# Two layer changes: three quarters of the layer norm's scaling on GpSimd, and other orders on ScalarE and VectorE

## The reference

```
def _layernorm(x, w, b):
    xf = x.astype(jnp.float32)
    mu = jnp.mean(xf, axis=-1, keepdims=True)
    var = jnp.mean(jnp.square(xf - mu), axis=-1, keepdims=True)
    return ((xf - mu) * lax.rsqrt(var + EPS)).astype(x.dtype) * w + b

for layer in range(DEPTH):
    y = _mla_mixer(x, ...) if layer % N_MIXERS == 0 else _mlstm_mixer(x, ...)
    x = _layernorm(ALPHA * x + y, ln_w[layer], ln_b[layer])
```

## Time and profile before

| What | us |
|---|---|
| median of 3 runs (1819.11 to 1819.42) | 1819.4 |
| the profiled execution's own time | 1819.39 |
| its span, first to last instruction | 1817.7 |
| TensorE busy in the span | 1803.0 |
| VectorE busy | 1270.0 |
| ScalarE busy | 942.8 |
| GpSimd busy | 37.8 |

### The profile page before, as it was taken

The page is one execution under the profiler, slowest core; times in us unless marked ns, Lnnn a source line. Parts: engine busy times, 40 slices in busy tenths (PEclk is TensorE's granted clock), DMA queues, the critical chain, the costliest instruction groups (busy, mean ns, idle before and its releaser), DMA issues.

```text
span 1817.7 us, 24358 instructions
## 1 busy us (share of the span) xinstructions
PE 1803.0 (99%) x8863; PEld 1518.4 (84%) x8863; DVE 1270.0 (70%) x1720; ACT 942.8 (52%) x1310; POOL 37.8 (2%) x116
## 2 busy tenths in 40 slices
PE   8999999999999999999999999999999999999999
PEld 7899998878888888887888888888878888888887
DVE  6766766588556755767887878787786556577764
ACT  4555554455465555636655545554454444565542
POOL 2000000000000004000000000000000000000000
PEclk9999999999999999999999999999999999999999
DMA  8554454668889887575555564544776776555453
GB/s 295 172 176 149 136 176 155 204 179 188 182 151 211 176 179 175 192 238 161 171 177 151 164 183 150 175 152 159 235 208 209 214 218 207 160 164 161 162 165 114
DMA packets 175067, 326.72 MB, mean 180 GB/s; under 512 B 16824, under 2 KB 24912, under 8 KB 174208
## 3 DMA queue, kind: packets, MB, share of 16 engines
q1 hardware_dynamic: 173840, 321.04, 61.6%
q10 hardware_dynamic: 576, 4.19, 0.6%
q0 software_dynamic: 560, 0.26, 0.1%
HBM read 319.68 MB, written 5.77 MB: 179 GB/s over the span
## 4 chain that ended last, share of the span: by engine, by line
PE 98%; DVE 1%; ACT 1%; issue 0%; DMA 0%; DVEq 0%
PE acc L388 28%; PE acc L390 28%; PE acc L389 28%; PE ps L650 2%; PE ps L2921 2%; PE ps L498 1%; PE acc L354 1%; PE acc L355 1%; PE acc L353 1%; PE ps L683 1%; PE acc L341 0%; PE acc L371 0%; PE acc L372 0%; PE acc L375 0%; PE acc L377 0%; PE acc L370 0%
## 5 line engine op out<-in xcount | busy, mean ns | idle before, releaser
L324 DVE TENSOR_TENSOR wsp<-wraw,wsp 128x1024 fp32r<-128x1024 f32 x576 | 696.6, 1224 | 334.1 <-ACT wsp L304 331.3
L304 ACT ACTIVATE wsp<-wraw 128x1024 fp32r<-128x1024 f32 x576 | 597.6, 1053 | 369.7 <-PE acc L390 337.4
L388 PE MATMUL acc<-wsp,ta 128*128 128x512 f32 x1664 | 659.3, 396 | 4.5 <-DVE wsp L324 2.4
L390 PE MATMUL acc<-wsp,ta 128*128 128x512 f32 x1664 | 649.2, 390 | 0.0
L389 PE MATMUL acc<-wsp,ta 128*128 128x512 f32 x1664 | 647.7, 389 | 0.0
L388 PEld LDWEIGHTS acc<-wsp,ta 128*128 128x128 f32 x1664 | 312.6, 188 | 69.8 <-issue 4.3
L390 PEld LDWEIGHTS acc<-wsp,ta 128*128 128x128 f32 x1664 | 312.3, 188 | 66.8
L389 PEld LDWEIGHTS acc<-wsp,ta 128*128 128x128 f32 x1664 | 312.8, 188 | 62.4
L388 PE MATMUL acc<-wsp,tb_hi 128*128 128x512 f32 x576 | 228.2, 396 | 0.0
L390 PE MATMUL acc<-wsp,tb_lo 128*128 128x512 f32 x576 | 224.8, 390 | 0.0
L389 PE MATMUL acc<-wsp,tb_hi 128*128 128x512 f32 x576 | 224.4, 390 | 0.0
(11 more groups left out here) (334 smaller groups left out, 1585.2 us busy)
## 6 DMA issues: line engine op xcount, KB each, us to landing
wraw<-in_ml_w_in SPq DMA_DIRECT2D x129, 512.0 KB, 5.7
wraw<-in_a_w_in SPq DMA_DIRECT2D x128, 512.0 KB, 3.8
wraw<-in_kv_w SPq DMA_DIRECT2D x64, 512.0 KB, 4.4
wraw<-in_b_w_in SPq DMA_DIRECT2D x64, 512.0 KB, 4.3
wraw<-in_mla_w_in SPq DMA_DIRECT2D x49, 512.0 KB, 4.6
wraw<-in_mla_w_out SPq DMA_DIRECT2D x32, 512.0 KB, 4.1
wraw<-in_ml_w_out SPq DMA_DIRECT2D x32, 512.0 KB, 4.6
wraw<-in_a_w_out SPq DMA_DIRECT2D x32, 512.0 KB, 4.0
```

The costliest lines, as they stand in the source:

```text
L304: nc.scalar.activation(unit_of(whi, n, SPLIT, w), unit_of(wraw, n, RAW, w), ACT.Copy).then_inc(w_high, 1)
L324: nc.vector.tensor_tensor(unit_of(wlo, n, SPLIT, w), unit_of(wraw, n, RAW, w), unit_of(whi, n, SPLIT, w).bitcast(F32), ALU.subtract).then_ ...
L388: nc.tensor.matmul(o, xh, wh, start=first, stop=False)
L390: m = nc.tensor.matmul(o, xl, wh, start=False, stop=end)
```

## The change

Both layer changes are edited alike; the arithmetic is the same.

- `ln_scale` on VectorE now does quarter 0 only. A new `ln_scale` on GpSimd does quarters 1 to 3 as three instructions of 128x512, each raising the new semaphore `xn_rest`; it waits for `nrm_a`. GpSimd does (0, 0) and (0, 1) ahead of its pads and mask, and (1, 0) and (1, 1) behind the masks of the third layer.
- TensorE's `ln_turn` waits for `xn_ok` for quarter 0 and for `xn_rest` for quarters 1 to 3. `ln_stream` waits for both.
- ScalarE makes the high half of unit 2 behind hi(0, 0) instead of ahead of affine(0, 0).
- VectorE does `ln_stats` of block 1 behind the low half of unit 2, directly ahead of `ln_scale(n, 1)`, instead of between unit 1 and lo(0, 1); the scale of quarters 1 to 3 of block 1, which stood behind unit 3, is gone from its queue.
- In `head_norm` of the last layer two semaphores become one; ScalarE's wait has the same meaning.

```diff
--- before.py
+++ after.py
@@ -163,6 +163,7 @@
         lnp_in = sem("lnp_in")
 
         nrm_a, nrm_v, xn_ok = sem("nrm_a"), sem("nrm_v"), sem("xn_ok")
+        xn_rest = sem("xn_rest")
         st_out = sem("st_out")
 
 
@@ -969,7 +970,7 @@
 
 
 
-        l3 = sems(3, "r_dg r_row f_row f_e f_ok sq_out x_sq x_out x_in x_tmp x_hi x_lo kss qss oss ksq kv_ krs kn kt kT qsq qv qrs qn qt qT sc msk mx ex pt ptc pv o "
+        l3 = sems(3, "r_dg r_row f_row f_e f_ok sq_out x_sq x_out x_in x_tmp x_hi x_lo ksq kv_ krs kn kt kT qsq qv qrs qn qt qT sc msk mx ex pt ptc pv o "
                      "ge gs sq v rs on og ogp tmp hi lo")
 
         def dst_l3(name, k, b, it):
@@ -1189,6 +1190,17 @@
                 pool.dma_start(gbias[:, 1:2], a["kv_f_bias_2"].rearrange("(n o) -> n o", o=1)).then_inc(bias_in, 16)
             pool.dma_start(posi, a["positions"][0:1, :].to_broadcast([P, T])).then_inc(bias_in, 16)
 
+            def ln_scale(n, b):
+
+
+                pool.wait_ge(nrm_a, 2 * n + b + 1)
+                for q in range(1, 4):
+                    x = x_res[:, b, q * COLS:(q + 1) * COLS]
+                    nc.gpsimd.tensor_scalar(x, x, mv[:, b, 0:1], nrm[:, b, 2:3], ALU.subtract,
+                                            ALU.mult).then_inc(xn_rest, 1)
+
+            ln_scale(0, 0)
+            ln_scale(0, 1)
             pool.wait_ge(xn_ok, 1)
             own.mark(nc.gpsimd.memset(cin[:, :, 0:PAD], 0.0))
             own.mark(nc.gpsimd.memset(mask[:], 0.0))
@@ -1223,6 +1235,9 @@
                 nc.gpsimd.tensor_copy(lvl[:, i, :].rearrange("p (m t) -> p m t", t=P),
                                       lvf.unsqueeze(1).to_broadcast([P, 4, P])).then_inc(l2["masks"], 1)
                 pool.wait_ge(l2["masks"], i + 2)
+
+            ln_scale(1, 0)
+            ln_scale(1, 1)
 
 
         @block.scalar
@@ -1358,10 +1373,11 @@
                 hi = lambda b, q: ln_hi(act, own, turn, b, q)
                 split = lambda p: step(act, high, evac, name, p)
                 ln_rstd(n, 0)
-                for p in range(3):
+                for p in range(2):
                     split(p)
                 affine(0, 0)
                 hi(0, 0)
+                split(2)
                 hi(0, 1)
                 affine(0, 2)
                 split(3)
@@ -1627,7 +1643,7 @@
                 nc.scalar.activation(ps2(2), src.rearrange("p b n -> p (b n)"), ACT.Square).then_inc(done, 1)
 
             def inverse_root(v, rs, g):
-                act.wait_ge(v, g + 1)
+                act.wait_ge(v, 2 * g + 2)
                 nc.scalar.activation(sm[:, 40:48], sm[:, 32:40], ACT.Ln).then_inc(rs, 1)
                 act.wait_ge(rs, 2 * g + 1)
                 nc.scalar.activation(sm[:, 48:56], sm[:, 40:48], ACT.Exp, scale=-0.5).then_inc(rs, 1)
@@ -1883,9 +1899,9 @@
 
             quarter = lambda q0, q1: slice(q0 * COLS, q1 * COLS)
 
-            def ln_scale(n, b, q0, q1):
-
-                c = quarter(q0, q1)
+            def ln_scale(n, b):
+
+                c = quarter(0, 1)
                 dve.wait_ge(nrm_a, 2 * n + b + 1)
                 nc.vector.tensor_scalar(x_res[:, b, c], x_res[:, b, c], mv[:, b, 0:1], nrm[:, b, 2:3],
                                         ALU.subtract, ALU.mult).then_inc(xn_ok, 1)
@@ -1896,7 +1912,8 @@
                 half = len(pieces) // 2
                 if i == 0:
                     dve.wait_ge(lnp_in, 32 * (n + 1))
-                    dve.wait_ge(xn_ok, 4 * n + 4)
+                    dve.wait_ge(xn_ok, 2 * n + 2)
+                    dve.wait_ge(xn_rest, 6 * n + 6)
                 piece = lambda j: (pieces[j][0], quarter(pieces[j][1], pieces[j][1] + 1))
                 if i > 0:
                     own.sync()
@@ -2031,20 +2048,18 @@
                 split = lambda p: step(dve, low, evac, name, p)
                 last_residual(done, 0)
                 ln_stats(n, done, 0)
-                ln_scale(n, 0, 0, 1)
-                ln_scale(n, 0, 1, 4)
+                ln_scale(n, 0)
                 split(0)
                 affine(0, 1)
                 last_residual(done, 1)
                 lo(0, 0)
                 split(1)
-                ln_stats(n, done, 1)
                 lo(0, 1)
                 split(2)
-                ln_scale(n, 1, 0, 1)
+                ln_stats(n, done, 1)
+                ln_scale(n, 1)
                 lo(0, 2)
                 split(3)
-                ln_scale(n, 1, 1, 4)
                 lo(0, 3)
                 lo(1, 0)
                 affine(1, 1)
@@ -2494,12 +2509,12 @@
                                                       ALU.add))
                 nc.vector.tensor_copy(negF, frow[:, 3, :]).then_inc(l3["f_ok"], 1)
 
-            def head_norm(dst, src, sq, ss, vs, rs, on, g):
+            def head_norm(dst, src, sq, vs, rs, on, g):
 
                 dve.wait_ge(sq, g + 1)
                 nc.vector.tensor_reduce(sm[:, 32:40], ps2(2).rearrange("p (n d) -> p n d", d=HD), AX,
-                                        ALU.add).then_inc(ss, 1)
-                dve.wait_ge(ss, g + 1)
+                                        ALU.add).then_inc(vs, 1)
+                dve.wait_ge(vs, 2 * g + 1)
                 nc.vector.tensor_scalar(sm[:, 32:40], sm[:, 32:40], 1.0 / HD, EPS, ALU.mult, ALU.add).then_inc(vs, 1)
                 dve.wait_ge(rs, 2 * g + 2)
                 for b in range(TB):
@@ -2548,7 +2563,7 @@
 
             def kv_side(g, p):
                 if p == late("l3_kv", 0):
-                    head_norm(qw3, qw3, l3["ksq"], l3["kss"], l3["kv_"], l3["krs"], l3["kn"], g)
+                    head_norm(qw3, qw3, l3["ksq"], l3["kv_"], l3["krs"], l3["kn"], g)
                     if not first(g):
                         dve.wait_ge(l3["kT"], 64 * g)
                     blocks = square_blocks(o3.rearrange("p b n -> p (b n)"))
@@ -2579,7 +2594,7 @@
             def q_side(g, u):
 
                 def norm():
-                    head_norm(qw3, qw3, l3["qsq"], l3["qss"], l3["qv"], l3["qrs"], l3["qn"], g)
+                    head_norm(qw3, qw3, l3["qsq"], l3["qv"], l3["qrs"], l3["qn"], g)
 
                 def out_(hh):
                     r = fox.inverse(dve, own, g, hh)
@@ -2593,7 +2608,7 @@
                     nc.vector.tensor_tensor(gw3[:, b, :], gw3[:, b, :], tmpT[:, 0, :], ALU.mult).then_inc(l3["gs"], 1)
 
                 def post():
-                    head_norm(o3, o3, l3["sq"], l3["oss"], l3["v"], l3["rs"], l3["on"], g)
+                    head_norm(o3, o3, l3["sq"], l3["v"], l3["rs"], l3["on"], g)
                     dve.wait_ge(l3["on"], 2 * g + 2)
                     dve.wait_ge(l3["gs"], 2 * g + 2)
                     flat = lambda v: v.rearrange("p b n -> p (b n)")
@@ -2755,7 +2770,10 @@
                 l0_side(3, p, l0_at("l0_out"))
             def ln_turn(n, b, q):
 
-                pe.wait_ge(xn_ok, 4 * n + 2 * b + (1 if q == 0 else 2))
+                if q == 0:
+                    pe.wait_ge(xn_ok, 2 * n + b + 1)
+                else:
+                    pe.wait_ge(xn_rest, 6 * n + 3 * b + q)
                 turn_block(x_res, b, q, n == 1 and b == 1)
 
             def ln_change(n, done, src, name):
```

## The result

The changed kernel takes **1825.69 us** (median of 7, 1825.53 to 1827.23) against 1819.42: ratio 1.0037, 95% interval 1.0027 to 1.0046. That is 6.3 us slower, above the predicted range of 1817.3 to 1823.2, and on the side of the slower rival. In the changed kernel's code all lines lie a little further down: 498 is 499, 324 is 325, 555 is 556, 583 is 584, VectorE's scale 1890 is 1906, and GpSimd's scale is 1199.

What follows compares the result with a forecast made beforehand. TensorE was taken as the bound, busy 1803.0 of 1817.7 us, with 3.54 us of pauses to win; losses of 2 x (0.19 + 0.90) = +2.2 us on 1819.4 gave 1821.6 us, range 1817.3 to 1823.2.

Steps and rivals of the forecast that it cites:

- slower rival: Block 1 ahead of unit 3: GpSimd's quarter is long, 1.16 us and fully blocked, +5.0 us, 1824.4; chance 0.14.
- ScalarE's order and VectorE until unit 2: First layer change: affine(0, 0) at 357.15, TensorE resumes at 360.40 instead of 360.94, unit 2 1.39 us earlier.
- The 0.19 stays: Unit 3 in block 1: TensorE follows at 367.03 against 366.84, so 0.19 us is lost per change, 0.38 in both.
- After this point TensorE has no wait: After unit 3 in either change: no TensorE wait today and nothing else late, so the 0.19 us loss remains.
- I take 0.61, the same shape on the same engine: GpSimd's 128x512 scale, without a trace row: assumed 0.61 us, as GpSimd's cast of 128x512.
- my upper bound of 1.16: GpSimd's 128x512 scale: at most 1.16 us, from four selects of 128x128 at 0.29 each.
- signs of being wrong: Layer changes: unit 3 no later and TensorE's idle falling, or quarters above 0.9 us and transposes waiting for GpSimd.
- Hidden, also at 0.9 us each: Block 0: GpSimd's quarters end near 356.1, 357.9 and 358.5, before TensorE wants them at about 357.0, 358.9 and 359.4.
- The collisions: Block 1, before lo(0, 2) and unit 3: GpSimd holds VectorE up twice at 0.45 us, 0.90 per change.
- the sum of 1821.6: Whole kernel: 2 x (0.19 + 0.90) = +2.2 us on 1819.4 us.
- the select's cost per element: GpSimd's select of 128x128 at 0.29 us, the evidence for a 1.16 us quarter and a kernel time of 1824.4.
- the prediction's own case: Both layer changes: GpSimd quarters of 0.61 us, two collisions of 0.45 per change, +2.2 us; chance 0.50.

Runs made afterwards that it cites:

- experiment 3: Kernel before in its own ScalarE and VectorE orders, with the scale of quarters 1 to 3 moved to GpSimd: 1825.68 us, ratio 1.0034.
- the copies: Changed kernel with GpSimd's scale of quarters 1 to 3 replaced by a copy of each quarter onto itself: 1824.49 us, ratio 1.0027.

## Why the prediction was wrong, point by point

- **ScalarE's order and VectorE until unit 2: right.** With the orders alone, 360.40 for TensorE's return and 367.05 for new(0, 3) were as worked out.
- **"The 0.19 stays": wrong, small.** The orders alone cost nothing. "After this point TensorE has no wait" overlooked that new(1, 0) hung on lo(1, 0) already, which ended at 369.7; 0.19 of slack was there. What the prediction left out is that the later root also delays GpSimd: with the three long quarters behind it, the new orders cost 1.5 us (experiment 3).
- **"I take 0.61, the same shape on the same engine": the step that failed.** Same shape, another operation. The quarter is 2.06 us, and my upper bound of 1.16 was itself built from other operations (selects). The quarters above 0.9 us and the transposes waiting for GpSimd are what the prediction had named as signs of being wrong. With 2.06, block 0's last quarter comes 6.5 us after the root where it is wanted after 4.4, and "Hidden, also at 0.9 us each" falls.
- **The collisions: right as a mechanism, mis-sized both ways.** With short instructions they cost 1.2 us per change (0.90 forecast): three collisions instead of two, since VectorE's scale was held up as well, of 0.37 to 0.40 each instead of 0.45. The cast's own row had VectorE pay 0.31 of 0.45, which makes 0.42 of a whole one. So that the estimate of 1821.3 without the clock comes so near the sum of 1821.6 is in part luck: the third collision stands in for the 0.19 that wasn't there. With the long instructions only 0.41 was lost; presumably GpSimd reached just one border between VectorE's instructions before unit 3, which no run tests. The Trainium skill (SBUF — State Buffer, Who interferes with whom) has the second instruction fully blocked. For the copies the rows go that way, with 0.37 to 0.40 of the 0.61. Beside the 2.06 us scale they don't: lo(0, 0) and unit 1 kept 0.68 and 1.22. Beside the scale of 128x1536 they do, at 5.43.
- **The slower rival: right side, wrong way.** I had priced it by VectorE being held up, 1824.4. What happened is that the transposes waited for GpSimd, which the prediction named only in a half-sentence. Its chance of 0.14 rested on the select's cost per element, which was the better row, though its 1.16 is little more than half of the 2.06 too.
- **The clock was not in the prediction at all.** It doesn't move the changed kernel's median, but it moves what came nearest to the prediction's own case by 2.9 us, and the medians of most trials.

The Trainium skill (GPSIMD Engine Reference, 4.1 Engine selection) has one-input operations on GpSimd "roughly line-rate". As an estimate from its 1.2 GHz that is 0.43 us and a dispatch; this case shows 1.68 to 2.08, and 0.61 for the copy alone.

## What to carry to other kernels

A duration carries over from one instruction to another only with the operation, not with shape and engine; where an engine has never run the operation, put one in an idle stretch and read it before moving work onto it. Work off the path may go to a slow engine only against a deadline per piece: here 2.3, 4.4 and 6.5 us against transposes that wanted the pieces after 2.0, 3.9 and 4.4. And a pause in the busiest engine is to be priced with what the clock may do behind it, not by its length alone. Last, two edits that are each measured alone don't add up: the orders cost nothing alone and 1.5 us once GpSimd's quarters hung on the root that they delay. And where executions of one kernel fall into groups, compare the groups and not the medians.

## What was not expected of the hardware

- A GpSimd tensor_scalar on float32 goes at about 3.0 to 4.0 ns per element and partition (128x512 in 2.06 us with operands by column, 1.93 with immediates, 1.68 with one operation), while a copy of 128x512 takes 0.61 us.
- TensorE's granted clock fell to half in eight of the eleven profiles of kernels with scaling or copying on GpSimd (for 3.4 or 6.8 us in the layer changes), and in none of the six without. In the layer changes it came behind pauses of 1.40 to 1.90 us, in 36 of the 52 executions of the kernels that have such pauses; in the 65 executions of the trials whose longest pause there was 1.12 or less it never came, also not with a quarter on GpSimd. The same kernel did it in one execution and not in the next. What decides it was not found.
- Beside GpSimd instructions of 128x1536, single VectorE instructions took 5.43 us instead of 0.28 and 4.35 instead of 1.22; beside the same operation on 128x512 VectorE ran freely most of the time (0.68 and 1.22 us for its two-input instructions at 360.13 and 360.73).
